# Routing of a grouped top-2 MoE on one core: fewer steps for group scores and counts, lists moved, router weights loaded a stage earlier

## The chip, the core and the metric

The kernel runs on one NeuronCore of a Trainium2 chip. The metric is device time of one execution in microseconds (us). Engines: TensorE (PE), VectorE (DVE), ScalarE (ACT), GpSimd (POOL) and SyncE (SP), each with its own instruction stream; they meet through semaphores.

## The reference

One inference step of a two-layer decoder trunk, all in fp32: a gated linear attention layer, then a differential attention layer, for 512 prompt tokens and 8 sample tokens together. Each layer ends with a mixture of experts of 16 experts in 4 groups, and this is what the change is about:

```python
probs = softmax((xt @ w_router + b_router).astype(float32), axis=-1)
pg = probs.reshape(-1, N_GROUPS, EXPERTS_PER_GROUP)          # 4 groups of 4
gscore = sum(lax.top_k(pg, 2)[0], axis=-1)                   # score of a group: its two best
gidx = argmax(gscore, axis=-1)
in_group = take_along_axis(pg, gidx[:, None, None], axis=1)[:, 0]
vals, idx = lax.top_k(in_group, 2)
wts = vals / sum(vals, axis=-1, keepdims=True)
...
for e in range(16):
    h = silu(xt @ w_gate[e]) * (xt @ w_up[e])
    y = y + comb[:, e:e + 1] * (h @ w_down[e])
```

## The kernel before

The kernel is a row of stages, each a block of one program per engine; a block ends with a barrier of all engines. Tokens lie in tiles of 128 partitions, NTT = 5 of them (four of the prompt, one with the 8 sample tokens). For each layer the stages around the change are the same: the mixer's output projection, `stage_modulate` (L339), `stage_route` (L1121), `stage_experts` (L1367), `stage_combine` (L1572).

`stage_modulate` scales and shifts the rows of each tile on VectorE (L377, L380), turns them on TensorE (L389), copies them on ScalarE (L399) and stores the rows from SP's queue (L359). Two row buffers take turns, so VectorE's tile i waits until the store of tile i - 2 has landed. SP first issues the loads of the gate rows (L335, L336). The argument `ahead` names further loads, which SP issues behind the gate rows and before the first row store; in this stage of before it is empty.

`stage_route` begins on SP with the router's weights (L1160, 64 bytes a piece) and bias (L1161), then the two vectors of the layer norm (L1162, L1163), then 2 MB each of gate, up and down weights of expert 0 and gate and up of expert 1 (L1117). TensorE waits for weights and bias, and for VectorE's memset of the weights' padding (L1235). It multiplies them with the tokens (L1195, four shares in parallel), ScalarE and VectorE take the shares out of PSUM, TensorE adds them (L1200). From there VectorE works through a chain of small instructions, nearly each followed by a drain (`tt`, L1229, is a TENSOR_TENSOR and a drain): softmax, group scores as the maximum over six pairs of experts (11 instructions), the mask of the best group (the last of its steps at L1279), first and second choice (O1, O2). Then choices are masked with `valid` (rows past the 8 sample tokens), summed to T, and added up tile by tile in `before`. TensorE turns the counts into each choice's rank within its expert (L1206 to L1209). VectorE works out how many tiles of 128 slots each expert needs (`nt`, L1298 to L1303) and where they start (a scan, L1306), and the slot of each choice (RK). Next come the lists for the expert stage, on one partition: which expert a late tile belongs to (`m.texp`), which tiles are more than half full (`m.full`), and how many pairs of tiles run; they are read by `stage_experts` only. Then the slots (`m.dest`), ten one-hot matrices (L1361), of which TensorE makes the token list as each comes (L1213), and the copy of that list, `m.idx` (L1364), which ends the stage.

`stage_experts` runs over slot tiles: GpSimd gathers the rows named in `m.idx` (L1420, L1423), TensorE turns them (L1436), multiplies with gate and up weights (L1488) and down weights (L1470). SP loads the weights for tile n once the gate and up product of tile n - 2 is done (L1117).

Of the kernel before, what the change touches and what calls it, by code (L numbers as in the profile page):

```python
# [1120 lines left out]
def stage_route(nc, ctx, m, l, a, weights):  # L1121
# [3 lines left out]
    w_in, ln_in, tab, mm, ev, sel_ok, rk_mm, hot_ok, idx_mm, tri_ok = (sem(n) for n in  # L1125
        ("w_in", "ln_in", "tab", "mm", "ev", "sel_ok", "rk_mm", "hot_ok", "idx_mm", "tri_ok"))
    ex_ok, wz_ok, sh_mm, sh_cp = (sem(n) for n in ("ex_ok", "wz_ok", "sh_mm", "sh_cp"))
    off = [2 * D]
# [5 lines left out]
    wr, br = take(KT, 32), take(1, NE)[:, 0, :]  # L1134
    shares = take(1, SEQ + 32)[:, 0, :]
    before = take(NTT + 1, NE)
    L, E, O1, O2, T, RK = (take(NTT, NE) for _ in range(6))
    GS, GM = take(NTT, NG), take(NTT, NG)
    A1, A2, A3 = (take(NTT, 1)[:, :, 0] for _ in range(3))
# [17 lines left out]
    with nc.Block() as block:  # L1157
        @block.sync
        def _(sp):
            sp.dma_start(wr[:, :, 0:NE], a["w_router"].rearrange("(p k) n -> p k n", k=KT)).then_inc(w_in, 16)  # L1160
            sp.dma_start(br, a["b_router"].partition_broadcast(P)).then_inc(w_in, 16)  # L1161
            sp.dma_start(m.lnr[:, 0, :], a["ln_ffn_g"][l].partition_broadcast(P)).then_inc(ln_in, 16)  # L1162
            sp.dma_start(m.lnr[:, 1, :], a["ln_ffn_b"][l].partition_broadcast(P)).then_inc(ln_in, 16)  # L1163
            load_expert(sp, m, weights, 0, 0)
            load_expert(sp, m, weights[0:2], 1, 1)
            sp.wait_ge(ln_in, 32)

        @block.gpsimd
        def _(g):
# [16 lines left out]
            nc.gpsimd.iota(row0, pattern=[[1, P]], base=-P, channel_multiplier=0, allow_small_or_imprecise_dtypes=True).then_inc(tab, 1)  # L1186

        @block.tensor
        def _(pe):
            pe.wait_ge(w_in, 32)  # L1190
            pe.wait_ge(wz_ok, 1)
            for k in range(KT):
                g = k % 4
                for bank, t0, n in ((m.ps[0], 0, SEQ), (m.ps[1], SEQ, 32)):
                    last = nc.tensor.matmul(bank[32 * g:32 * g + 32, 0:n], wr[:, k, :], m.xt[:, k, t0:t0 + n],  # L1195
                                            start=(k < 4), stop=(k >= 4), tile_position=(0, 32 * g))
            last.then_inc(sh_mm, 1)
            pe.wait_ge(sh_cp, 2)
            for i, r in TILES:
                last = nc.tensor.matmul(m.ps[2][0:r, i * NE:(i + 1) * NE], shares[:, i * P:i * P + r], m.fold[:, 0:NE],  # L1200
                                        start=True, stop=True)
            last.then_inc(mm, 1)
            pe.wait_ge(sel_ok, 1)
            pe.wait_ge(tab, 10)

            nc.tensor.matmul(m.ps[3][:, 0:NTT * NE], m.ones[:, :], before[:, 0:NTT, :].rearrange("p i e -> p (i e)"),  # L1206
                             start=True, stop=False)
            nc.tensor.matmul(m.ps[3][:, 0:NTT * NE], tri, T.rearrange("p i e -> p (i e)"), start=False, stop=True)
            last = nc.tensor.matmul(m.ps[5][:, 0:NE], m.ones[:, :], before[:, NTT, :], start=True, stop=True)  # L1209
# [15 lines left out]
        def _(v):  # L1225
# [11 lines left out]
            V.memset(before[:, 0, :], 0.0)  # L1237
# [21 lines left out]
            pairs = [(x, y) for x in range(EPG) for y in range(x + 1, EPG)]  # L1259
# [4 lines left out]
            v.wait_ge(tab, 10)  # L1264
# [12 lines left out]
            tt(E.rearrange("p i (g e) -> p i g e", e=EPG), e4, GM.unsqueeze(3).to_broadcast([P, NTT, NG, EPG]), ALU.mult)  # L1277
            tt(E.rearrange("p i (g e) -> p i g e", e=EPG), e4, GM.unsqueeze(3).to_broadcast([P, NTT, NG, EPG]), ALU.add)
            V.tensor_scalar(E, E, -1.0, None, ALU.add)  # L1279
# [10 lines left out]
            tt(O1, O1, bc(valid), ALU.mult)  # L1290
            tt(O2, O2, bc(valid), ALU.mult)
            tt(T, O1, O2, ALU.add)
            for i in range(NTT):
                tt(before[:, i + 1, :], before[:, i, :], T[:, i, :], ALU.add)
            v.nop().then_inc(sel_ok, 1)
            v.wait_ge(rk_mm, 1)

            V.tensor_scalar(nt, m.ps[5][:, 0:NE], float(P), None, ALU.is_gt)  # L1298
            v.drain()
            for c in range(2, NTT):  # L1300
                V.tensor_scalar(tmp16, m.ps[5][:, 0:NE], float(c * P), None, ALU.is_gt)
                v.drain()
                tt(nt, nt, tmp16, ALU.add)  # L1303
            V.memset(zero16, 1.0)
# [13 lines left out]
            tt(RK, RK, far, ALU.add)  # L1318

# [25 lines left out]
            for c, O in enumerate((O1, O2)):  # L1345
                tt(O, O, RK, ALU.mult)
                V.tensor_reduce(out=slot[:, c, :], in_=O, axis=AX.X, op=ALU.add)
                v.drain()
                V.tensor_copy(m.dest[:, c, :], slot[:, c, :])
            slot1 = slot.rearrange("p c i -> p (c i)")  # L1350
            tt(reached, slot1.unsqueeze(2).to_broadcast([P, NJ, SLOT_TILES + 1]),
               tile0.unsqueeze(1).to_broadcast([P, NJ, SLOT_TILES + 1]), ALU.is_ge)
            V.tensor_reduce(out=row, in_=reached, axis=AX.X, op=ALU.add)
            V.tensor_tensor(token_at, reached[:, :, 0:SLOT_TILES], reached[:, :, 1:SLOT_TILES + 1], ALU.subtract)

            tt(tok, tok, valid, ALU.mult)
            V.scalar_tensor_tensor(out=row, in0=row, scalar=float(-P), in1=slot1, op0=ALU.mult, op1=ALU.add)
            by_choice = token_at.rearrange("p (c i) t -> p c i t", i=NTT)
            tt(by_choice, by_choice, tok.unsqueeze(1).unsqueeze(3).to_broadcast([P, 2, NTT, SLOT_TILES]), ALU.mult)
            for j in range(NJ):  # L1360
                V.tensor_scalar(row_hot[:, j, :], row0, row[:, j:j + 1], None, ALU.is_equal).then_inc(hot_ok, 1)  # L1361

# [1048 lines left out]
def build(nc, a):  # L2411
    held.clear()
    with ExitStack() as ctx:
# [46 lines left out]
```

## Time and profile before

| | us |
|---|---|
| median of three runs | 2049.24 |
| lowest and highest of them | 2048.81 and 2052.35 |
| the profiled execution | 2054.24 |
| its span in the trace | 2052.4 |

| engine | busy us | share of the span |
|---|---|---|
| PE | 1583.4 | 77% |
| PEld (weight load, beside PE) | 729.2 | 36% |
| DVE | 753.0 | 37% |
| ACT | 390.5 | 19% |
| POOL | 364.8 | 18% |

HBM traffic is 274 GB/s over the span. Times of the trace are microseconds from the start of the span. Layer 0's modulation begins at about 500 us and its routing at 516, layer 1's routing at 1583. A row of the timeline gives the start, the duration, the engine, the line, the operation with its tiles and shapes, and how many instructions it merges; in brackets stands the engine's idle time before it and what ended it. A drain isn't counted as busy, so the time from one start to the next is more than the duration where a drain lies between, and can be less where none does. PEclk is TensorE's granted clock as a share of 2.4 GHz, so 0.50 is 1.2 GHz. The DMA share is the mean busy share of the core's 16 DMA engines.

### The profile page before, as it was taken

To read this page: it belongs to the slowest core of one execution; us is meant where nothing else is said; L and a number is where in the kernel's file an instruction comes from. 1 tells how busy PE (TensorE), PEld (TensorE's weight loads), DVE (VectorE), ACT (ScalarE), POOL (GpSimd) and SP (SyncE) were. 2 spreads that over 40 slices of the span, in tenths; PEclk is the share of its full clock that TensorE was granted. 3 is DMA by queue.
4 is the path that set the end of the run, shared out by engine and by line. 5 is a ranking of instruction groups with operands and counts; after the bars stand their busy time and mean duration, and the time that the engine had idled before them with its cause. 6 is when DMAs were issued, how large, how long until landed. Compare 5 with 4: busy or idle time off the path is not lost. (4 is left out here: it accounts for less than half of the span.)

```text
span 2052.4 us, 22129 instructions
## 1 busy us (share of the span) xinstructions
PE 1583.4 (77%) x7466; PEld 729.2 (36%) x7467; DVE 753.0 (37%) x1314; ACT 390.5 (19%) x755; POOL 364.8 (18%) x274
## 2 busy tenths in 40 slices
PE   6999976786288998946889887777495399989950
PEld 2333335233133333312346563344342233333320
DVE  1010134575400000036755568995455400000008
ACT  1010022011022122222120002333211011222212
POOL 0000000001010000023735566650001000000004
PEclk8989987588589999977999998889796599999985
DMA  8652620611589989969969999884402579999972
GB/s 330 256 198 84 245 84 12 229 71 52 238 329 428 376 352 425 427 275 328 362 225 378 405 389 411 336 319 139 185 21 82 224 291 386 409 428 428 428 296 92
DMA packets 122909, 563.03 MB, mean 274 GB/s; under 512 B 13621, under 2 KB 43126, under 8 KB 101307
## 3 DMA queue, kind: packets, MB, share of 16 engines
q1 hardware_dynamic: 98450, 496.63, 61.0%
q10 hardware_dynamic: 15424, 33.08, 4.2%
q0 software_dynamic: 8944, 32.15, 4.2%
q8 instruction: 51, 0.84, 0.2%
q14 instruction: 40, 0.33, 0.0%
HBM read 521.80 MB, written 40.03 MB: 274 GB/s over the span
## 5 line engine op out<-in xcount | busy, mean ns | idle before, releaser
L1488 PE MATMUL ps<-arena_w,arena_r 128*64 128x512 f32 x1664 | 378.6, 612 | 33.5 <-issue 28.5
L1488 PEld LDWEIGHTS ps<-arena_w,arena_r 128*64 128x64 f32 x1664 | 126.4, 141 | 279.4 <-issue 273.3
L1470 PE MATMUL ps<-arena_w,arena_r 128*64 128x512 f32 x832 | 186.9, 597 | 19.2 <-ACT arena_r L1518 19.2
L1565 DVE TENSOR_TENSOR arena_r<-arena_r,ps 128x512 f32<-128x512 f32 x38 | 26.2, 688 | 441.9 <-ACT arena_r L1535 441.9
L1868 POOL TENSOR_TENSOR arena_w<-arena_w,arena_r 128x1024 f32<-128x1024 f32 x48 | 116.4, 2430 | 112.5 <-DMA arena_w<-in_cache_k_dram 111.9
L1921 PE MATMUL ps<-arena_w,xt 128*128 128x256 f32 x512 | 124.3, 405 | 1.4 <-ACT xt L2086 1.4
L1868 POOL TENSOR_TENSOR arena_r<-arena_r 128x1024 f32<-128x1024 f32 x48 | 115.0, 2400 | 48.9 <-DMA arena_r<-in_cache_k_dram 48.8
L512 PE MATMUL ps<-arena_w,xt 128*128 128x512 f32 x256 | 113.6, 601 | 0.4 <-PE ps L206 0.4
L1091 POOL TENSOR_TENSOR x_res<-x_res,arena_m 128x1024 f32<-128x1024 f32 (+1 forms) x20 | 52.6, 2631 | 341.6 <-DVE x_res L1085 341.6
L1022 PE MATMUL ps<-arena_w,xt 128*128 128x512 f32 x256 | 111.1, 593 | 0.0
L1921 PEld LDWEIGHTS ps<-arena_w,xt 128*128 128x128 f32 x512 | 103.0, 204 | 18.2 <-ACT xt L2086 1.5
L1420 POOL COPY small<-idx 128x1 int32 (+1 forms) x38 | 6.9, 183 | 567.2 <-PE ps L1436 485.5
L1470 PEld LDWEIGHTS ps<-arena_w,arena_r 128*64 128x64 f32 x832 | 56.8, 137 | 123.1 <-issue 101.4
L1558 DVE COPY arena_r<-ps 128x512 f32<-128x512 f32 x38 | 26.3, 692 | 192.1 <-PE ps L1470 192.1
L1534 ACT ACTIVATE arena_r<-ps 64x512 f32<-64x512 f32 x38 | 22.4, 588 | 360.3 <-PE ps L1488 360.3
L2237 DVE TENSOR_REDUCE arena_r<-arena_w 128x16 f32<-128x1024 f32 x64 | 76.8, 1213 | 25.9 <-POOL arena_w L1868 25.8
L2237 DVE TENSOR_REDUCE arena_r<-arena_r 128x16 f32<-128x1024 f32 x64 | 76.6, 1210 | 16.5 <-POOL arena_r L1868 16.5
L1933 PE MATMUL ps<-arena_m,arena_r 128*16 128x512 f32 x512 | 68.8, 661 | 6.1 <-DMA arena_m<-in_cache_v_dram 6.1
L512 PEld LDWEIGHTS ps<-arena_w,xt 128*128 128x128 f32 x256 | 48.3, 192 | 66.7 <-issue 66.7
L1022 PEld LDWEIGHTS ps<-arena_w,xt 128*128 128x128 f32 x256 | 48.2, 190 | 60.0 <-issue 58.4
L471 PE MATMUL ps<-xt,arena_w 128*128 128x512 f32 x128 | 58.7, 612 | 4.0 <-PEq L248 3.7
L1913 PE MATMUL ps<-xt,arena_w 128*128 128x512 f32 x128 | 60.3, 630 | 0.0
(355 smaller groups left out, 1959.1 us busy)
## 6 DMA issues: line engine op xcount, KB each, us to landing
arena_w<-in_w_exp_gate_dram SPq DMA_DIRECT2D x38, 2048.0 KB, 13.4
arena_w<-in_w_exp_up_dram SPq DMA_DIRECT2D x38, 2048.0 KB, 17.2
arena_w<-in_w_exp_down_dram SPq DMA_DIRECT2D x38, 2048.0 KB, 18.9
arena_m<-in_cache_v_dram SPq DMA_DIRECT2D x128, 512.0 KB, 8.3
arena_w<-in_cache_k_dram SPq DMA_DIRECT2D x64, 512.0 KB, 8.3
arena_r<-in_cache_k_dram SPq DMA_DIRECT2D x64, 512.0 KB, 9.8
arena_w<-in_w_ada_dram SPq DMA_DIRECT2D x12, 2048.0 KB, 16.8
arena_m<-in_w_ada_dram SPq DMA_DIRECT2D x12, 2048.0 KB, 8.5
```

The source lines that it names most:

```text
L471: last = nc.tensor.matmul(m.ps[n % 2][:, :], w, m.xt[:, k, 0:SEQ], start=(k == 0), stop=(k == KT - 1))
L512: last = nc.tensor.matmul(m.ps[4 + n % 4][:, :], m.xt[:, k, i * P:(i + 1) * P], m.wr[c % 2][:, k, :], start=(k == 0), stop=(k == KT - 1))
L1022: last = nc.tensor.matmul(m.ps[(4 if n % 2 else 6) + c][0:r, :], m.xt[:, k, i * P:i * P + r], w[:, k, c * 512:(c + 1) * 512], start=(k == ...
L1091: nc.gpsimd.tensor_tensor(m.x[0:r, i, :], m.x[0:r, i, :], m.lnr[0:r, 1, :], ALU.add).then_inc(self.done, 1)
L1470: last = nc.tensor.matmul(psy[c][at:at + 64, :], ht[u][:, k, 64 * (1 - a):64 * (2 - a)], wd[u][:, k, c * 512:(c + 1) * 512], start=(k == 0 ...
L1488: last = nc.tensor.matmul(ps[at:at + 64, :], xgt[u][:, k, 64 * a:64 * (a + 1)], w[u][:, k, :], start=(k == 0), stop=(k == KT - 1), tile_po ...
L1558: V.tensor_copy(ys[u][:, 0:512], psy[0][:, :]).then_inc(y_v, 1)
L1868: G.tensor_tensor(kp[n % RING], kp[n % RING], qb[b % 2], ALU.mult).then_inc(pp_ok, 1)
L1913: last = nc.tensor.matmul(bank[:, :], w[:, k, part * P:(part + 1) * P], m.xt[:, k, 0:SEQ], start=(k == 0), stop=(k == KT - 1))
L1921: last = nc.tensor.matmul(bank[:, i * CW:(i + 1) * CW], m.xt[:, k, t], w[:, k, :], start=(k == 0), stop=(k == KT - 1))
L1933: last = nc.tensor.matmul(PSO[n][32 * g:32 * g + C, :], PR[b % 2][:, GRP * q + g, :], vp[GRP * (v % 2) + g][:, n * 512:(n + 1) * 512], sta ...
L2237: V.tensor_reduce(out=S[b % 2][:, j, :], in_=kp[n % RING].rearrange("p (c d) -> p c d", d=DHB), axis=AX.X, op=ALU.add).then_inc(ks_ok, 1)
```

## The change

Six edits, all for both layers.

- A class `Router` holds the router's weights, bias and their semaphore. Their two loads move from the head of `stage_route` into `stage_modulate`'s `ahead`.
- Group scores: within each group, two couples of experts; the larger of each couple, added, against the larger of the two couples' sums. Five instructions, two of them not followed by a drain, take the place of eleven.
- The mask's last step is folded into the one before it.
- T is masked once in place of O1 and O2. `before` is now laid out with tiles innermost, and one TENSOR_TENSOR_SCAN over 16 x 6 elements fills it; a table `fresh` restarts it for each expert. TensorE reads `before` and the masked T with a stride.
- `nt` comes from one comparison with a table `steps` and one reduction. The table is one more iota on POOL; three more memsets stand at the head of VectorE's part, and one there moves from the chain.
- The block of the lists for the expert stage stands behind the one-hot matrices and before the wait for the token list.

```diff
+class Router:
+    def __init__(self, nc, ctx, m, l, a):
+        self.w_in = ctx.enter_context(m_semaphore(nc, f"route{l}_w_in"))
+        self.wr, self.br = view(m.R, 2 * D, KT, 32), m.R[:, 2 * D + KT * 32:2 * D + KT * 32 + NE]
+        self.ahead = [(self.wr[:, :, 0:NE], a["w_router"].rearrange("(p k) n -> p k n", k=KT), self.w_in),
+                      (self.br, a["b_router"].partition_broadcast(P), self.w_in)]
...
         @block.sync
         def _(sp):
-            sp.dma_start(wr[:, :, 0:NE], a["w_router"].rearrange("(p k) n -> p k n", k=KT)).then_inc(w_in, 16)
-            sp.dma_start(br, a["b_router"].partition_broadcast(P)).then_inc(w_in, 16)
...
-            nc.tensor.matmul(m.ps[3][:, 0:NTT * NE], m.ones[:, :], before[:, 0:NTT, :].rearrange("p i e -> p (i e)"),
+            nc.tensor.matmul(m.ps[3][:, 0:NTT * NE], m.ones[:, :], before[:, :, 0:NTT].rearrange("p e i -> p i e"),
                              start=True, stop=False)
...
-            V.memset(before[:, 0, :], 0.0)
+            V.memset(chosen, 0.0)
+            V.memset(fresh, 1.0)
+            v.drain()
+            V.memset(fresh[:, :, 0:1], 0.0)
+            V.memset(zero16, 1.0)
...
-            for n, (x, y) in enumerate(pairs):
-                tt(G3 if n else GS, e4[:, :, :, x], e4[:, :, :, y], ALU.add)
-                if n:
-                    tt(GS, GS, G3, ALU.max)
+            V.tensor_tensor(hi, two[:, :, :, 0], two[:, :, :, 1], ALU.max)
+            tt(both, two[:, :, :, 0], two[:, :, :, 1], ALU.add)
+            V.tensor_tensor(gs, hi[:, :, 0], hi[:, :, 1], ALU.add)
+            tt(g3, both[:, :, 0], both[:, :, 1], ALU.max)
+            tt(gs, gs, g3, ALU.max)
...
-            V.tensor_scalar(E, E, -1.0, None, ALU.add)
+            V.scalar_tensor_tensor(out=e4, in0=GM.unsqueeze(3).to_broadcast([P, NTT, NG, EPG]), scalar=-1.0, in1=e4,
+                                   op0=ALU.add, op1=ALU.add)
...
-            tt(O1, O1, bc(valid), ALU.mult)
-            tt(O2, O2, bc(valid), ALU.mult)
             tt(T, O1, O2, ALU.add)
-            for i in range(NTT):
-                tt(before[:, i + 1, :], before[:, i, :], T[:, i, :], ALU.add)
-            v.nop().then_inc(sel_ok, 1)
+            tt(taken, T, bc(valid), ALU.mult)
+            V.tensor_tensor_scan(before.rearrange("p e i -> p (e i)"), fresh.rearrange("p e i -> p (e i)"),
+                                 chosen.rearrange("p e i -> p (e i)"), 0.0, ALU.mult, ALU.add).then_inc(sel_ok, 1)
+            v.drain()
             v.wait_ge(rk_mm, 1)
 
-            V.tensor_scalar(nt, m.ps[5][:, 0:NE], float(P), None, ALU.is_gt)
-            v.drain()
-            for c in range(2, NTT):
-                V.tensor_scalar(tmp16, m.ps[5][:, 0:NE], float(c * P), None, ALU.is_gt)
-                v.drain()
-                tt(nt, nt, tmp16, ALU.add)
-            V.memset(zero16, 1.0)
+            tt(over, m.ps[5][:, 0:NE].unsqueeze(2).to_broadcast([P, NE, NTT - 1]), steps.unsqueeze(1).to_broadcast([P, NE, NTT - 1]),
+               ALU.is_gt)
+            V.tensor_reduce(out=nt, in_=over, axis=AX.X, op=ALU.add)
             v.drain()
...
-            one = cmp_[0:1, 0:MORE, :]
-            tt(one, end[0:1].unsqueeze(1).to_broadcast([1, MORE, NE]), tix[0:1, 0:MORE].unsqueeze(2).to_broadcast([1, MORE, NE]), ALU.is_le)
...
-            V.tensor_copy(m.texp[0:1, SLOT_TILES:SLOT_TILES + 1], tmp16[0:1, 0:1])
             for c, O in enumerate((O1, O2)):
                 tt(O, O, RK, ALU.mult)
...
             for j in range(NJ):
                 V.tensor_scalar(row_hot[:, j, :], row0, row[:, j:j + 1], None, ALU.is_equal).then_inc(hot_ok, 1)
 
+            one = cmp_[0:1, 0:MORE, :]
+            tt(one, end[0:1].unsqueeze(1).to_broadcast([1, MORE, NE]), tix[0:1, 0:MORE].unsqueeze(2).to_broadcast([1, MORE, NE]), ALU.is_le)
...
+            V.tensor_copy(m.texp[0:1, SLOT_TILES:SLOT_TILES + 1], tmp16[0:1, 0:1])
             v.wait_ge(idx_mm, 1)
             V.tensor_copy(m.idx[:, :], m.ps[4][:, 0:SLOT_TILES])
...
-        stage_modulate(nc, ctx, m, "ffn0", 3, 3, have=2, keep_rows=True)
+        router = Router(nc, ctx, m, 0, a)
+        stage_modulate(nc, ctx, m, "ffn0", 3, 3, have=2, keep_rows=True, ahead=router.ahead)
         weights = expert_weights(nc, ctx, m, 0, a)
-        stage_route(nc, ctx, m, 0, a, weights)
+        stage_route(nc, ctx, m, 0, a, weights, router)
```

## Rows read from the trace of the kernel before

**Rows 1.** Windows of layer 0: us of each engine, clock, DMA share, GB/s
```profile
515.90:557.00 41.10, 11.02 (x68) 8.03 (x68) 21.01 (x107) 2.14 (x3) 1.39 (x12) 0.54 0.70 283
...
547.00:548.00 1.00, 0.00 (x0) 0.00 (x0) 0.78 (x6) 0.00 (x0) 0.00 (x0) 0.50 0.08 33
...
576.30:620.00 43.70, 36.24 (x174) 15.29 (x174) 4.13 (x6) 12.09 (x23) 3.60 (x7) 0.96 0.99 404
```

**Rows 2.** Timeline, routing of layer 0: start, duration, engine, operation [idle before]
```profile
515.92 0.56 SPq L1160 DMA_DIRECT2D arena_r<-in_w_router_dram  x1
...
516.01 0.17 DVE L1235 MEMSET arena_r<- 128x128 f32 x1 [2.31 <-PEq L347]
...
517.23 0.59 SPq L1162 DMA_DIRECT2D arena_m<-in_ln_ffn_g_dram  x1
...
519.38 3.89 PE L1195 MATMUL ps<-xt,arena_r 128*32 128x512 f32 x32 [4.59 <-DMA arena_r<-in_b_router_dram]
...
523.99 1.20 PE L1200 MATMUL ps<-fold,arena_r 128*128 128x16 f32 x10 [0.71 <-ACT arena_r L1220]
```

**Rows 3.** Timeline, routing of layer 1
```profile
1586.70 3.89 PE L1195 MATMUL ps<-xt,arena_r 128*32 128x512 f32 x32 [4.66 <-DMA arena_r<-in_b_router_dram]
...
1591.31 2.04 PE L1200 MATMUL ps<-fold,arena_r 128*128 128x16 f32 x10 [0.72 <-ACT arena_r L1220]
```

**Rows 4.** Timeline, modulation of layer 0
```profile
502.97 11.04 SPq L359 DMA_DIRECT2D xm_rows<-arena_r  x5
...
505.92 1.23 DVE L377 SCALAR_TENSOR_TENSOR arena_r<-arena_m,x_res 128x1024 f32<-128x1024 f32 x1 [0.53 <-DMA xm_rows<-arena_r]
```

**Rows 5.** Windows: the queue before the row store; router weights alone
```profile
503.30:503.70 0.40, 0.40 (x3) 0.40 (x2) 0.40 (x1) 0.00 (x0) 0.00 (x0) 0.50 0.28 113
...
517.00:518.30 1.30, 0.00 (x0) 0.00 (x0) 0.00 (x0) 0.00 (x0) 0.37 (x3) 0.50 0.59 60
```

**Rows 6.** Timeline, selection and counts, layer 0
```profile
527.13 3.13 DVE L1229 TENSOR_TENSOR arena_r<-arena_r 128x80 f32<-128x80 f32 x12
...
532.22 0.20 DVE L1279 TENSOR_SCALAR arena_r<-arena_r 128x80 f32<-128x80 f32 x1
...
537.20 2.12 DVE L1229 TENSOR_TENSOR arena_r<-arena_r 128x80 f32<-128x80 f32 x8
...
539.40 0.71 PE L1206 MATMUL ps<-arena_r,ones 128*128 128x80 f32 x2 [14.21 <-DVEq L1230]
```

**Rows 7.** Timeline, VectorE behind the counts' products, layer 0
```profile
540.90 0.17 DVE L1298 TENSOR_SCALAR arena_r<-ps 128x16 f32<-128x16 f32 x1 [1.58 <-PE ps L1209]
...
542.84 0.19 DVE L1306 TENSOR_TENSOR_SCAN arena_r<-arena_r 128x16 f32<-128x16 f32 x1
...
543.36 0.24 DVE L1310 TENSOR_SCALAR arena_r<-ps 128x80 f32<-128x80 f32 x1
...
543.51 0.17 DVE L1311 SCALAR_TENSOR_TENSOR arena_r<-arena_r 128x16 f32<-128x16 f32 x1
```

**Rows 8.** Timeline, lists, one-hot rows and token list, layer 0
```profile
544.15 0.91 DVE L1229 TENSOR_TENSOR arena_r<-arena_r 128x80 f32<-128x80 f32 x3
...
548.24 0.22 DVE L1229 TENSOR_TENSOR arena_r<-arena_r 128x80 f32<-128x80 f32 x1
...
551.55 2.05 DVE L1361 TENSOR_SCALAR arena_r<-arena_r 128x128 f32<-128x128 f32 x10
...
556.39 0.18 DVE L1364 CAST idx<-ps 128x24 int32<-128x24 f32 x1 [2.79 <-PE ps L1213]
```

**Rows 9.** Timeline, first products of layer 0's expert stage
```profile
566.55 8.65 PE L1488 MATMUL ps<-arena_w,arena_r 128*64 128x512 f32 x28 [1.16 <-ACT arena_r L1512]
...
576.27 0.36 SPq L1117 DMA_DIRECT2D arena_w<-in_w_exp_gate_dram  x1
...
578.45 7.09 PE L1488 MATMUL ps<-arena_w,arena_r 128*64 128x512 f32 x32 [1.31 <-ACT arena_r L1512]
```

**Rows 10.** Groups by line: the other scan, busy us, mean ns
```profile
L650 DVE TENSOR_TENSOR_SCAN arena_r<-arena_r 128x512 f32<-128x512 f32 x4 | 4.9, 1214 | 0.0
```

More of the change, by code:

```diff
@@ L1118, in load_expert, with stage_route @@
                      source[bass.ds(e, 1)].rearrange("a (p k) n -> p (a k n)", k=k)).then_inc(loaded[u], 16)
-def stage_route(nc, ctx, m, l, a, weights):
+class Router:
[4 more added lines that the diff above has]
+                      (self.br, a["b_router"].partition_broadcast(P), self.w_in)]
+def stage_route(nc, ctx, m, l, a, weights, router):
     sem = lambda n: ctx.enter_context(m_semaphore(nc, f"route{l}_{n}"))
-    w_in, ln_in, tab, mm, ev, sel_ok, rk_mm, hot_ok, idx_mm, tri_ok = (sem(n) for n in
-        ("w_in", "ln_in", "tab", "mm", "ev", "sel_ok", "rk_mm", "hot_ok", "idx_mm", "tri_ok"))
+    ln_in, tab, mm, ev, sel_ok, rk_mm, hot_ok, idx_mm, tri_ok = (sem(n) for n in
+        ("ln_in", "tab", "mm", "ev", "sel_ok", "rk_mm", "hot_ok", "idx_mm", "tri_ok"))
+    w_in, wr, br = router.w_in, router.wr, router.br
     ex_ok, wz_ok, sh_mm, sh_cp = (sem(n) for n in ("ex_ok", "wz_ok", "sh_mm", "sh_cp"))
-    off = [2 * D]
+    off = [2 * D + KT * 32 + NE]
     def take(*shape):
@@ L1133, in take @@
         return v
-    wr, br = take(KT, 32), take(1, NE)[:, 0, :]
     shares = take(1, SEQ + 32)[:, 0, :]
-    before = take(NTT + 1, NE)
     L, E, O1, O2, T, RK = (take(NTT, NE) for _ in range(6))
+    before, fresh, chosen = (take(NE, NTT + 1) for _ in range(3))
+    taken = chosen[:, :, 1:].rearrange("p e i -> p i e")
     GS, GM = take(NTT, NG), take(NTT, NG)
+    HI, PS = take(2 * NTT, NG), take(2 * NTT, NG)
+    over, steps = take(NE, NTT - 1), take(1, NTT - 1)[:, 0, :]
     A1, A2, A3 = (take(NTT, 1)[:, :, 0] for _ in range(3))
@@ L1186, in _ @@
             nc.gpsimd.iota(row0, pattern=[[1, P]], base=-P, channel_multiplier=0, allow_small_or_imprecise_dtypes=True).then_inc(tab, 1)
+            nc.gpsimd.iota(steps, pattern=[[P, NTT - 1]], base=P, channel_multiplier=0, allow_small_or_imprecise_dtypes=True).then_inc(tab, 1)
         @block.tensor
@@ L1203, in _ @@
             pe.wait_ge(sel_ok, 1)
-            pe.wait_ge(tab, 10)
-            nc.tensor.matmul(m.ps[3][:, 0:NTT * NE], m.ones[:, :], before[:, 0:NTT, :].rearrange("p i e -> p (i e)"),
+            pe.wait_ge(tab, 11)
+            nc.tensor.matmul(m.ps[3][:, 0:NTT * NE], m.ones[:, :], before[:, :, 0:NTT].rearrange("p e i -> p i e"),
                              start=True, stop=False)
-            nc.tensor.matmul(m.ps[3][:, 0:NTT * NE], tri, T.rearrange("p i e -> p (i e)"), start=False, stop=True)
-            last = nc.tensor.matmul(m.ps[5][:, 0:NE], m.ones[:, :], before[:, NTT, :], start=True, stop=True)
+            nc.tensor.matmul(m.ps[3][:, 0:NTT * NE], tri, taken, start=False, stop=True)
+            last = nc.tensor.matmul(m.ps[5][:, 0:NE], m.ones[:, :], before[:, :, NTT], start=True, stop=True)
             last.then_inc(rk_mm, 1)
@@ L1258, in _ @@
             e4 = E.rearrange("p i (g e) -> p i g e", e=EPG)
-            pairs = [(x, y) for x in range(EPG) for y in range(x + 1, EPG)]
-            for n, (x, y) in enumerate(pairs):
-                tt(G3 if n else GS, e4[:, :, :, x], e4[:, :, :, y], ALU.add)
-                if n:
-                    tt(GS, GS, G3, ALU.max)
-            v.wait_ge(tab, 10)
+            two = E.rearrange("p i (g q e) -> p (i g) q e", q=2, e=2)
+            hi, both = (x.rearrange("p i g -> p (i g)").rearrange("p (n q) -> p n q", q=2) for x in (HI, PS))
+            gs, g3 = (x.rearrange("p i g -> p (i g)") for x in (GS, G3))
+            V.tensor_tensor(hi, two[:, :, :, 0], two[:, :, :, 1], ALU.max)
[3 more added lines that the diff above has]
+            tt(gs, gs, g3, ALU.max)
+            v.wait_ge(tab, 11)
             def first_of(onehot, score, best, weights, n):
@@ L1275, in _ @@
             first_of(GM, GS, A1, w4, NG)
[L1277 to L1279 removed]
+            tt(e4, e4, GM.unsqueeze(3).to_broadcast([P, NTT, NG, EPG]), ALU.mult)
+            V.scalar_tensor_tensor(out=e4, in0=GM.unsqueeze(3).to_broadcast([P, NTT, NG, EPG]), scalar=-1.0, in1=e4,
+                                   op0=ALU.add, op1=ALU.add)
             v.drain()
@@ L1318, in _ @@
             tt(RK, RK, far, ALU.add)
+            for c, O in enumerate((O1, O2)):
+                tt(O, O, RK, ALU.mult)
+                V.tensor_reduce(out=slot[:, c, :], in_=O, axis=AX.X, op=ALU.add)
+                v.drain()
+                V.tensor_copy(m.dest[:, c, :], slot[:, c, :])
+            slot1 = slot.rearrange("p c i -> p (c i)")
+            tt(reached, slot1.unsqueeze(2).to_broadcast([P, NJ, SLOT_TILES + 1]),
+               tile0.unsqueeze(1).to_broadcast([P, NJ, SLOT_TILES + 1]), ALU.is_ge)
+            V.tensor_reduce(out=row, in_=reached, axis=AX.X, op=ALU.add)
+            V.tensor_tensor(token_at, reached[:, :, 0:SLOT_TILES], reached[:, :, 1:SLOT_TILES + 1], ALU.subtract)
+            tt(tok, tok, valid, ALU.mult)
+            V.scalar_tensor_tensor(out=row, in0=row, scalar=float(-P), in1=slot1, op0=ALU.mult, op1=ALU.add)
+            by_choice = token_at.rearrange("p (c i) t -> p c i t", i=NTT)
+            tt(by_choice, by_choice, tok.unsqueeze(1).unsqueeze(3).to_broadcast([P, 2, NTT, SLOT_TILES]), ALU.mult)
+            for j in range(NJ):
+                V.tensor_scalar(row_hot[:, j, :], row0, row[:, j:j + 1], None, ALU.is_equal).then_inc(hot_ok, 1)
             one = cmp_[0:1, 0:MORE, :]
@@ L1344, in _ @@
             V.tensor_copy(m.texp[0:1, SLOT_TILES:SLOT_TILES + 1], tmp16[0:1, 0:1])
[L1345 to L1361, printed above, removed]
             v.wait_ge(idx_mm, 1)
@@ L2434, in build @@
                          (a["ln_mix_g"][1], a["ln_mix_b"][1]), 8, 9, w_at=8192)
-        stage_modulate(nc, ctx, m, "ffn1", 9, 3, have=2, keep_rows=True)
+        router = Router(nc, ctx, m, 1, a)
+        stage_modulate(nc, ctx, m, "ffn1", 9, 3, have=2, keep_rows=True, ahead=router.ahead)
         weights = expert_weights(nc, ctx, m, 1, a)
-        stage_route(nc, ctx, m, 1, a, weights)
+        stage_route(nc, ctx, m, 1, a, weights, router)
         stage_experts(nc, ctx, m, 1, weights)
```

## The prediction

> **What bounds the kernel now.** I read three views in this order. First the stages. The kernel is a row of stages with barriers between them. Layer 0's routing stage is a stretch of 41 us with TensorE at 11 us of work and VectorE at 21 us [rows 1]. Nothing is large there: it is a chain of small dependent instructions, and its length goes into the span in full if the stage behind it waits for its end. Second, the timeline of that stretch: what starts it, what each link costs from start to start, and where VectorE stands idle [rows 2, 3, 6 to 8]. Third, whether the expert stage behind would absorb a shorter routing. Expert weights preloaded by routing have landed by 547 us (DMA share 0.08 from there) [rows 1], but the first product needs the token list, which is ready at 556.4 [rows 8], and runs from 566.55; SP asks for the next weights only when that product is done, at 576.27 [rows 9]. From there DMA is 0.99 busy [rows 1]. So the DMA-bound part begins when routing lets it, and every microsecond taken out ahead of the token list moves it. Both layers have the same chain; I cost layer 0 and double it.
>
> **Part A, router weights loaded by the modulation stage.** Before, TensorE's first routing product starts at 519.38 behind the bias load, and VectorE's memset, its other condition, is done at 516.18 [rows 2]; in layer 1, where it starts at 1586.70, TensorE idles 4.66 us for the same load, against 4.59 [rows 2, 3]. Without the loads the product follows the memset by some 0.05 us: 519.38 - 516.23 = 3.15 us. VectorE now does two more memsets and a drain behind the first one; they lie beside the 3.89 us of products [rows 2], as does the added iota on POOL, which has 20 us until its tables are used.
>
> What the moved step costs in its new place: two issues on SP, 0.61 + 0.70 us from start to start [rows 2], ahead of the first row store at 502.97, which waits for VectorE anyway [rows 4]. In the code SP has only two gate-row loads ahead of it, so I let the issues fit. Their packets then lie on SP's queue ahead of that store. The router weights are 1024 pieces of 64 bytes; where they are alone, the engines are 0.59 busy for 1.3 us, so 0.77 us of work [rows 5], and the bias (an eighth of the pieces) some 0.2. The queue has a gap of 0.4 us at share 0.28 before the store, worth 0.29 us [rows 5]. VectorE waits 0.53 us for this store's landing before its third tile [rows 4], so a late store delays the stage one for one. Delay: 0.97 - 0.29 = 0.7; in layer 1 the gap is thinner, so I take 0.8. Ends: 0 (the pieces go into other unused slots) and 1.4 (the 1.3 us of wall time plus a bit of bias, no overlap). In return SP reaches the gain vectors and expert weights 1.3 us sooner (517.23 against 515.92) [rows 2], of no value with the slack of 9 us found above. **A = 3.15 - 0.8 = 2.35.**
>
> The Trainium skill ("DMA: Bandwidth & Descriptors", section "Queues, rings and completion order") says that each DMA engine takes its descriptors in ring order. By that rule the store can't pass the router pieces, and the delay is nearer 1.0 than 0; if it were fully serial, the total below would be 0.4 us smaller in all.
>
> **Part B, couples in place of pairs.** Twelve drained TENSOR_TENSORs take 3.13 us, 0.26 each [rows 6]; eleven are the six pairs: 2.87. In their place stand five, of which two are followed with no drain. A drained 40- or 20-element one costs 0.28 and 0.26 twice; an undrained one starts its follower after 0.15 us at 80 elements (543.36 to 543.51) [rows 7], so about 0.10 and 0.08 here. 2.87 - 0.98 = **1.89**. Ends: 2.0, and 1.53 if the undrained ones cost full price.
>
> [...]
>
> **Part C**, one TENSOR_SCALAR folded into a neighbour: 0.20 us, and a gap of 0.08 as between the last drained one (537.20 + 2.12) and what follows it at 539.40 [rows 6]: **0.28**.
>
> **Part D, one scan for the counts.** From 537.20 eight drained operations run until TensorE starts at 539.40: 2.20 us [rows 6]. After: two 80-element ones (three of about that size take 0.91, so 0.31 each [rows 8]), one now with a strided output, and one scan over 96 elements. A scan over 16 takes 0.19 and starts at 542.84 [rows 7], one over 512 takes 1.21 [rows 10]: 2.06 ns an element, so 0.36. With 0.08 to TensorE: 1.06. **D = 1.14**, between 0.95 and 1.3. TensorE's operands are now strided; I take nothing for it (up to 0.15).
>
> **Part E, tiles of an expert.** From 540.90 to the scan at 542.84: 1.94 us for seven small operations and a memset [rows 7]. After: one 64-element comparison and one reduction, both drained: 0.29 each. **E = 1.36** (1.3 to 1.45).
>
> **Part F, late tiles' lists moved.** They begin with the third operation of the group at 544.15, so at 544.77, and end at 548.24 [rows 8]: 3.47 us on the chain. Behind the ten one-hot rows VectorE stands idle 2.79 us until TensorE's twenty products are done at 556.39 [rows 8]. The lists start at about 553.55 and end at 553.55 + 3.47 = 557.02, so the copy of the token list, queued behind them, comes 0.63 us later than TensorE would let it. What is late next is therefore VectorE, not TensorE. The stage's barrier and then the gathers wait for it; the cover is worth 2.8 us, and were it gone the move would bring nothing. **F = 3.47 - 0.63 = 2.84** (2.6 to 3.0).
>
> **Sum.** 2.35 + 1.89 + 0.28 + 1.14 + 1.36 + 2.84 = 9.86 a layer, 19.7 for two. The profiled execution took 2054.24 us (span 2052.4), 5 us above the median of three, 2049.24. It would come to 2034.5, the median to 2049.24 - 19.7 = **2029.5**. By the lower ends (A 1.75, B 1.53, C 0.2, D 0.95, E 1.3, F 2.6) the gain is 8.3 a layer, 16.7 in all; by the upper ones (3.15, 2.0, 0.3, 1.3, 1.45, 3.0) it is 11.2, 22.4 in all.
>
> **Rivals.**
> 1. *TensorE's clock rises sooner.* Routing runs mostly at 1.2 GHz, half clock: 0.54 granted over the stretch [rows 1]. The ten fold products take 2.04 us in layer 1 and 1.20 in layer 0 [rows 3, 2], where the clock came up to 2.4 GHz while they ran. With the 3 us wait gone the first products follow the transposes of modulation more closely. At most 3.89 / 2 = 1.95 a layer and 0.84 for layer 1: 4.7 more, 2024.8. The opposite, layer 0 losing its 0.84, gives 2030.3. In layer 0 the clock came up only when the 32 products that started at 519.38 were through, and in layer 1 not even in the fold products [rows 2, 3], so the early rise is unlikely.
> 2. *The expert stage absorbs it.* If the stream of weights set its pace from the preload on, only SP's earlier start would count, 1.3 - 0.8 = 0.5 a layer, or 1.3 at most: 2046.6 to 2048.2, no change. Against it stand the quiet queue after 547 and the load that waits for the first product [rows 1, 9].
> 3. *The lists are not hidden.* If VectorE's lists delayed the row products too, or ran much slower next to TensorE, F is 0: 2029.5 + 5.7 = 2035.2. Their order in the code speaks against it. The whole change doing nothing would need this and 2.
> 4. *Slower: the clock in the expert stage.* That stage starts at half clock and comes to 0.96 within two tiles [rows 1, 9]. A gate-and-up product of 32 matmuls takes 7.09 us at full clock [rows 9], 14.2 at half. If the changed phase and shorter activity ahead held the clock down, each tile would lose 7.1 us where TensorE is the bound. The gain is eaten from three such tiles (21.3), and it is slower by over 0.2% from four: 2029.5 + 28.4 = 2057.9. Against it stands the 0.96 granted over the 43.7 us from 576.3, after a routing stage that was mostly idle too [rows 1].
>
> **Numbers.** Forecast with its bounds 0.80; rival 1 0.09; rival 2 0.03; rival 3 0.05; rival 4 0.03. The median of three also moves by a microsecond or two (2048.81 to 2052.35 before). Ends: 2049.24 - 22.4 - 2 = 2024.8, which takes in rival 1, rounded to 2024; and 2049.24 - 16.7 + 2 to 3, which takes in rival 3: 2036. About 0.2%, 4.1 us, is what a measurement tells from no change. Faster 0.94 (forecast, rivals 1 and 3), same 0.03, slower 0.03.
>
> **What would show it.** A: the first product some 0.2 us behind the stage's start, and VectorE's wait for the first row store up from 0.53 to about 1.3 us. If it stays at 0.5, A is 3.15. B to E: 0.98 us from the normalised probabilities to the reduction; one scan of 0.36; two operations of 0.58 ahead of the second scan. F: the last list operation, not TensorE, releases the token list, and idle time there is gone. From the token list to the first product and the end of the expert stage all times are as before, less the shift; an expert stage that is longer by what routing lost would prove rival 2, and a longer stretch at 0.5 in it rival 4. I am wrong above all if routing is shorter by 10 us a layer and the span isn't by 20.

## The result and the profile after

| | before | after |
|---|---|---|
| median of four runs, us | 2050.8 | 2033.49 |
| lowest to highest | 2048.81 to 2053.67 | 2031.04 to 2035.83 |
| ratio of runs, 95% interval | | 0.9908 (0.9887 to 0.9929) |
| a second series of the same kernel, five rounds: median | 2057.19 | 2032.99 |
| its ratio, 95% interval | | 0.9881 (0.9855 to 0.9907) |
| profiled execution (its span) | 2054.24 (2052.4) | 2031.04 (2029.2) |

Forecast were 2029.5 us and 19.7 us of gain. Measured are 17.3 us between the medians of the first series and 24.2 between those of the second. The interval of the first series is 14.6 to 23.2 us. The totals of one kernel scatter by several microseconds, so they can't tell 17 from 22. The traces can: VectorE's links of the routing chain repeat to a few hundredths, apart from short idle gaps of some 0.3 to 0.4 us. Four other links move from one execution to the next, and are named where they matter: modulation (by up to 0.8 us in layer 1), the first routing products (by 0.2 in layer 0), the fold products of layer 1 (1.20 or 2.04), and the last stretch to the first expert product (by 0.3).

The head of layer 0's routing stage after the change, in the timeline of all engines (start, duration, engine, line, operation, idle before). It answers [rows 2].

```profile
513.83 0.34 SPq L1172 DMA_DIRECT2D arena_m<-in_ln_ffn_g_dram  x1
513.92 0.17 DVE L1246 MEMSET arena_r<- 128x128 f32 x1 [2.32 <-PEq L347]
...
514.23 3.76 PE L1206 MATMUL ps<-xt,arena_r 128*32 128x512 f32 x32 [1.54 <-DVE arena_r L1246]
...
518.73 1.20 PE L1211 MATMUL ps<-fold,arena_r 128*128 128x16 f32 x10 [0.73 <-ACT arena_r L1231]
```

The first product now waits for VectorE's memset and starts 0.31 us behind the memset's start, where it was 3.37 behind in [rows 2]. The same view further on, for parts B to E; it answers [rows 6] and [rows 7].

```profile
521.87 0.24 DVE L1240 TENSOR_TENSOR arena_r<-arena_r 128x80 f32<-128x80 f32 x1
522.18 0.20 DVE L1277 TENSOR_TENSOR arena_r<-arena_r 128x40 f32<-128x40 f32 x1
522.30 0.19 DVE L1240 TENSOR_TENSOR arena_r<-arena_r 128x40 f32<-128x40 f32 x1
...
523.16 0.18 DVE L1286 TENSOR_REDUCE arena_r<-arena_r 128x5 f32<-128x20 f32 x1
...
529.83 0.62 DVE L1240 TENSOR_TENSOR arena_r<-arena_r 128x80 f32<-128x80 f32 x2
530.52 0.36 DVE L1310 TENSOR_TENSOR_SCAN arena_r<-arena_r 128x96 f32<-128x96 f32 x1
...
530.93 0.72 PE L1217 MATMUL ps<-arena_r,ones 128*128 128x80 f32 x2 [11.01 <-DVE arena_r L1310]
...
532.44 0.22 DVE L1240 TENSOR_TENSOR arena_r<-ps,arena_r 128x64 f32<-128x64 f32 x1 [1.56 <-PE ps L1220]
532.73 0.22 DVE L1317 TENSOR_REDUCE arena_r<-arena_r 128x16 f32<-128x64 f32 x1
533.03 0.19 DVE L1319 TENSOR_TENSOR_SCAN arena_r<-arena_r 128x16 f32<-128x16 f32 x1
```

The couples run from 522.18 to 523.16, 0.98 us for five. The scan over 96 elements takes the 0.36 us that the two others gave by a straight line. From the counts' products to VectorE's next step are 1.51 us, against 1.50 before (539.40 to 540.90): the strided operands of TensorE cost nothing that shows.

The end of the stage, VectorE alone but for two rows of other engines. It answers [rows 8] and the first row of [rows 9].

```profile
538.30 2.05 DVE L1349 TENSOR_SCALAR arena_r<-arena_r 128x128 f32<-128x128 f32 x10
538.64 4.46 PE L1224 MATMUL ps<-arena_r 128*128 128x24 f32 x20 [6.25 <-DVE arena_r L1349]
540.27 0.27 DVE L1240 TENSOR_TENSOR arena_r<-arena_r 1x128 f32<-1x128 f32 x1
...
543.66 0.14 DVE L1375 CAST texp<-arena_r 1x1 int32<-1x1 f32 x1
543.73 0.16 DVE L1377 CAST idx<-ps 128x24 int32<-128x24 f32 x1
...
553.84 9.47 PE L1501 MATMUL ps<-arena_w,arena_r 128*64 128x512 f32 x32 [1.16 <-ACT arena_r L1525]
```

The copy of the token list has no idle time before it any more. TensorE's products were through at 543.10; the lists, 3.46 us long, hold the copy until 543.73.

The chain cut at the same points in both kernels, start to start, from the timelines:

| stretch | layer 0 before | after | layer 1 before | after |
|---|---|---|---|---|
| modulation to the head of routing | 15.59 | 16.09 | 16.08 | 16.90 |
| to the first routing product | 3.37 | 0.31 | 3.46 | 0.31 |
| to the shares' copy | 3.97 | 3.86 | 3.97 | 3.95 |
| to the reciprocal (fold products, softmax) | 3.51 | 3.51 | 4.35 | 3.51 |
| to the first selection (part B) | 3.47 | 1.56 | 3.81 | 1.56 |
| to the counts' products (C, D) | 9.07 | 7.77 | 8.80 | 7.79 |
| to the scan for starts (E) | 3.44 | 2.10 | 3.44 | 2.09 |
| to the one-hot rows (F, the part saved) | 8.71 | 5.27 | 9.02 | 5.27 |
| to the copy of the token list (F, given back) | 4.84 | 5.43 | 4.84 | 5.43 |
| to the first expert product | 10.16 | 10.11 | 9.80 | 9.78 |
| **sum** | 66.13 | 56.01 | 67.57 | 56.59 |

The chains are shorter by 10.12 and 10.98 us, 21.1 in all. The spans of these two executions differ by 23.2: the part before layer 0's modulation is 2.6 us shorter in the one after, with nothing changed there, and the two other stretches (first expert product to layer 1's modulation, and from layer 1's first expert product to the end) are 0.4 and 0.1 longer.

### The profile page after: what moved, and what is told of

It reads as the page before. It is cut to its first block and busy times, and to the rows that moved or that the text cites. A ratio compares the mean times of both kernels' runs of the same rounds, so it can differ in the third digit from the quotient of the medians.

```text
span 2029.2 us, 22063 instructions
## 1 busy us (share of the span) xinstructions
PE 1577.2 (78%) x7466; PEld 725.8 (36%) x7467; DVE 748.1 (37%) x1284; ACT 390.9 (19%) x755; POOL 365.0 (18%) x276
## 5 line engine op out<-in xcount | busy, mean ns | idle before, releaser
L2250 DVE TENSOR_REDUCE arena_r<-arena_w 128x16 f32<-128x1024 f32 x64 | 76.8, 1212 | 23.2 <-POOL arena_w L1881 23.1
L2250 DVE TENSOR_REDUCE arena_r<-arena_r 128x16 f32<-128x1024 f32 x64 | 76.7, 1210 | 17.0 <-POOL arena_r L1881 16.9
## 6 DMA issues: line engine op xcount, KB each, us to landing
arena_w<-in_w_exp_gate_dram SPq DMA_DIRECT2D x38, 2048.0 KB, 14.6
```

Source lines behind the costliest of these rows:

```text
L2250: V.tensor_reduce(out=S[b % 2][:, j, :], in_=kp[n % RING].rearrange("p (c d) -> p c d", d=DHB), axis=AX.X, op=ALU.add).then_inc(ks_ok, 1)
```

## The experiments

The theory was that the routing chain goes into the span one for one, part by part as in the sum. The rival was that the expert stage gives some of it back. Each run was compared in its total and by the same stretches, with "chain" for the sum of both layers' chains. The 95% interval of a kernel's ratio reaches some 0.0026 to either side, which makes some 7.6 us for the difference of two kernels: the medians below agree or disagree with a theory only loosely, and the stretches decide. The same kernel run again has a chain of 55.94 + 56.07 = 112.0 us, and the one of the table above 112.6.

**again.** The changed kernel, unedited.

> The changed kernel as it is, for a closer ratio. Theory 1 (what leaves the routing chain leaves the span one for one): the two profiled executions differ by 10.1 us in layer 0 and 11.0 us in layer 1 between the start of modulation and the first expert product, so 21.1 us or a ratio of 0.9897. Theory 2 (the expert stage or a later one gives some of it back, since the medians of four runs differ by 17.3 us only): 0.9915 or closer to 1, and in the new profile a longer time from the first expert product to the end of the stage. In the trace: 56.0 and 56.6 us from the start of modulation to the first product.

Its ratio is 0.9881 (0.9855 to 0.9907), nearer to the first theory; 0.9897 lies within both series' intervals, 0.9915 only in the first one's. From the first expert product of layer 0 to the next modulation it takes 1000.7 us, before 1000.6: nothing is given back there.

**no_a.** Part A undone.

```diff
+            for buf, src, loaded in router.ahead:
+                sp.dma_start(buf, src).then_inc(loaded, 16)
             sp.dma_start(m.lnr[:, 0, :], a["ln_ffn_g"][l].partition_broadcast(P)).then_inc(ln_in, 16)
...
-        stage_modulate(nc, ctx, m, "ffn0", 3, 3, have=2, keep_rows=True, ahead=router.ahead)
+        stage_modulate(nc, ctx, m, "ffn0", 3, 3, have=2, keep_rows=True)
```

> The changed kernel with the router's loads back at the head of the routing stage, all else kept. Theory 1: the first routing product starts 3.4 us behind the stage's start again and modulation is shorter by 0.5 us in layer 0 and 0.8 us in layer 1, so 2.7 and 2.3 us more: 5.0 us above the changed kernel. If layer 1's fold products go back to 2.0 us from 1.2 as TensorE starts later behind the transposes (the clock), 5.9 us. Theory 2: about 2 us, the earlier issue of the expert weights alone.

Median 2037.79, 4.8 us above the changed kernel. Its chain is 118.3 us, 6.3 above the second execution of the changed kernel. 3.17 a layer came back at the products, 0.3 and 0.8 left modulation, 0.2 is the first products of layer 0 (3.97 from start to the copy, against 3.73), and 0.84 the fold products of layer 1. Expected were 5.0, or 5.9 with slow fold products. The timeline of TensorE in layer 1's routing, of this kernel:

```profile
1584.56 3.89 PE L1208 MATMUL ps<-xt,arena_r 128*32 128x512 f32 x32 [4.67 <-DMA arena_r<-in_b_router_dram]
...
1589.17 2.04 PE L1213 MATMUL ps<-fold,arena_r 128*128 128x16 f32 x10 [0.72 <-ACT arena_r L1233]
```

and of "again":

```profile
1572.34 3.89 PE L1206 MATMUL ps<-xt,arena_r 128*32 128x512 f32 x32 [1.50 <-DVE arena_r L1246]
...
1576.93 1.20 PE L1211 MATMUL ps<-fold,arena_r 128*128 128x16 f32 x10 [0.70 <-ACT arena_r L1231]
```

**no_f.** Part F undone: the block of lists stands ahead of the slots again.

> The changed kernel with the lists back ahead of the slots, all else kept. Theory 1: 3.45 us more ahead of the one-hot rows and 0.6 us less behind them, 2.85 a layer, 5.7 us in all; TensorE releases the token list again after 2.8 us of idle time. Theory 2: less than 3 us in all.

Median 2040.18, 7.2 above. The chain is 118.4, 6.4 above: 3.45 us more ahead of the one-hot rows and 0.59 less behind them in each layer, and again 0.84 of layer 1's fold products, which ran slow in this execution though the loads were early. The timeline of VectorE, layer 0:

```profile
544.35 2.05 DVE L1374 TENSOR_SCALAR arena_r<-arena_r 128x128 f32<-128x128 f32 x10
549.19 0.18 DVE L1377 CAST idx<-ps 128x24 int32<-128x24 f32 x1 [2.79 <-PE ps L1224]
```

The wait of 2.79 us for TensorE is back as in [rows 8]. 5.7 of 6.4 are what was expected of the part itself.

**no_bcde.** Parts B to E undone, with the five additions on the new layout. Of the edit, part D:

```diff
-            tt(T, O1, O2, ALU.add)
-            tt(taken, T, bc(valid), ALU.mult)
-            V.tensor_tensor_scan(before.rearrange("p e i -> p (e i)"), fresh.rearrange("p e i -> p (e i)"),
-                                 chosen.rearrange("p e i -> p (e i)"), 0.0, ALU.mult, ALU.add).then_inc(sel_ok, 1)
-            v.drain()
+            tt(O1, O1, bc(valid), ALU.mult)
+            tt(O2, O2, bc(valid), ALU.mult)
+            tt(taken, O1, O2, ALU.add)
+            for i in range(NTT):
+                tt(before[:, :, i + 1], before[:, :, i], chosen[:, :, i + 1], ALU.add)
+            v.nop().then_inc(sel_ok, 1)
```

> The changed kernel with the six pairs, the mask's third step, the five additions (on the new layout) and the seven small operations for tiles back, all else kept. Theory 1: 1.91 + 0.28 + 1.10 + 1.35 = 4.64 a layer, 9.3 us in all. Theory 2: less than 5 us in all. The additions read and write with a stride now; if a stride costs VectorE anything they take more than 0.26 us each from start to start.

Median 2037.04, only 4.1 above. That is the rival's side, but the theory's 9.3 is only 5.2 away and so within the 7.6 us too. The trace decides against the rival: the chain is 122.2, 10.2 above. B is 1.91 and 2.26 us, E 1.35 and 1.35, as expected, and C and D together 1.53 and 1.15; with 0.84 for the slow fold products. The execution profiled hides 5.5 of these 10.2 us in stretches that the edit doesn't touch: outside the chains it took 1912.2 us, and "again" 1917.7. Whether the other five runs did the same isn't known, as they have no trace. A stride costs VectorE little here: the eight operations with strided ones among them take 2.25 us, before 2.12 [rows 6].

**longer.** Time added to the chain.

```diff
             tt(taken, T, bc(valid), ALU.mult)
+            for _ in range(20):
+                tt(far, O1, O2, ALU.add)
```

> The changed kernel with twenty more drained operations of 128x80 on VectorE's chain, ahead of the counts (results overwritten later). Theory 1 (what the chain takes goes into the span one for one): 20 x 0.31 = 6.2 us a layer between the first selection and the counts' products, 12.4 us in all, and from the first expert product to the next stage no change beyond the scatter. Theory 2 (the expert stage absorbs a part, as its weights stream is the bound): less than 8 us in all, and a shorter stretch from the first expert product to the next layer's modulation.

Median 2047.22, 14.2 above the 2032.99 of "again", which was of another series; by the ratios (0.9967 against 0.9881 and 0.9908) it is 17.7 and 12.1 us. The group of operations in the timeline of VectorE, layer 0:

```profile
531.16 6.95 DVE L1240 TENSOR_TENSOR arena_r<-arena_r 128x80 f32<-128x80 f32 x22
```

Twenty more take 6.33 us (6.95 against 0.62), 12.7 in both layers, and the chain grew by 13.2: the fold products of layer 1 ran slow (0.84), and modulation took 0.2 less. From layer 0's first expert product to the next modulation it took 1001.2 us, against 1000.7: the expert stage absorbs nothing of a longer chain. With the 1000.7 of "again" against 1000.6 before, for a shorter one, this settles rival 2 of the prediction in both directions.

**behind.** The router's loads behind the first row store.

```diff
-            for buf, src, loaded in ahead:
-                sp.dma_start(buf, src).then_inc(loaded, 16)
             if keep_rows:
                 for i, r in TILES:
                     sp.wait_ge(xm_ok, i + 1)
                     sp.dma_start(m.xmD[i * P:i * P + r, :], xm[i % 2][0:r, :]).then_inc(rows_out[i % 2], 16)
+                    if i == 0:
+                        for buf, src, loaded in ahead:
+                            sp.dma_start(buf, src).then_inc(loaded, 16)
```

> The changed kernel with the router's two loads issued behind the first row store of modulation in place of ahead of it. Theory 1 (the store of tile 0 lies behind the router's pieces on SP's queue, and VectorE's third tile waits for it): VectorE's wait goes back from 1.0 and 1.9 us to 0.5 and 1.1, and modulation from 16.1 and 16.4 to 16.9 us back to 15.6 and 16.1, with the first routing product still 0.3 us behind the stage's start; 1.1 us less in all. Rival (the pieces cost engine time wherever they stand): the wait for the second row store, zero so far, grows to 0.5 us or more, and modulation stays at 16.1 us or above.

Modulation took 15.78 and 16.02 us. The starts of VectorE's first, third and fourth tile in layer 1, in the timeline of "behind":

```profile
1555.34 1.22 DVE L378 SCALAR_TENSOR_TENSOR arena_r<-arena_m,x_res 128x1024 f32<-128x1024 f32 x1
...
1558.85 1.23 DVE L378 SCALAR_TENSOR_TENSOR arena_r<-arena_m,x_res 128x1024 f32<-128x1024 f32 x1 [1.00 <-DMA xm_rows<-arena_r]
...
1561.69 1.23 DVE L378 SCALAR_TENSOR_TENSOR arena_r<-arena_m,x_res 128x1024 f32<-128x1024 f32 x1 [0.32 <-DMA xm_rows<-arena_r]
```

Both theories were half right. The wait for the first store is shorter (0.71 and 1.00), but the second store, free of any wait before, now makes VectorE wait 0.14 in layer 0 and 0.32 in layer 1; the wait for the last tile, 0.3 before, is 0.07 and 0. Median 2033.77, ratio 0.9904 (0.9872 to 0.9937): not to be told from the changed kernel by its total.

**actq.** The same loads from ScalarE's own queue; one execution.

```diff
-            for buf, src, loaded in ahead:
-                sp.dma_start(buf, src).then_inc(loaded, 16)
...
         @block.scalar
         def _(s):
+            for buf, src, loaded in ahead:
+                s.dma_start(buf, src).then_inc(loaded, 16)
```

> The changed kernel with the router's two loads issued by ScalarE, idle then, at the start of modulation, on its own DMA queue. Theory 1 (order on one queue makes the delay): modulation takes 15.6 and 16.1 us as before, or less than a quarter of a microsecond more. Rival (it is the engines' work that delays the store, whichever queue the pieces are on): 16.1 us and more, with VectorE's wait for the first row store at 1.0 us or above. What the late issue on SP costs in layer 1 (the bias load took SP 1.76 us, and the first store went out 0.5 us late) is gone under both.

Modulation took 15.98 and 17.00 us, with waits for the first row store of 0.93 and 1.98. In layer 1, timeline of VectorE:

```profile
1558.73 1.23 DVE L375 SCALAR_TENSOR_TENSOR arena_r<-arena_m,x_res 128x1024 f32<-128x1024 f32 x1 [1.98 <-DMA xm_rows<-arena_r]
```

The pieces stood on another queue, no store was behind them, and SP issued the first store on time. The store still landed late. So the order on one queue isn't needed for a delay; the rival, the work of the shared engines, fits. It is one execution, so the size stays rough, and the cause is argued by what is left over and not shown directly. Its total of 2027.77 us, the lowest of all here, tells nothing of the edit: its chain is 112.7 us, and outside the chains it took 1913.2.

**best.** The loads as in "behind", and the lists with independent steps side by side: five drains in place of ten (the expectation miscounts them as six and twelve).

```diff
+            V.tensor_tensor(one, wide(end), tall, ALU.is_le)
+            V.scalar_tensor_tensor(out=lim[0:1], in0=m.ps[5][0:1, 0:NE], scalar=1.0 / P, in1=start[0:1], ...)
+            V.tensor_scalar(tef[0:1, MORE:MORE + half], tix[0:1, 0:MORE:2], end[0:1, NE - 1:NE], None, ALU.is_lt)
+            v.drain()
+            V.tensor_reduce(out=tef[0:1, 0:MORE], in_=one, axis=AX.X, op=ALU.add)
...
```

> The changed kernel with the loads behind the first row store and the lists written so that independent steps stand side by side: six drains in place of twelve, with undrained neighbours. Theory 1: 0.5 and 0.6 us less in modulation; the lists take 2.4 us in place of 3.47 and so fit into the 2.8 us in which TensorE makes the token list, which TensorE then releases again: 4.84 us from the first one-hot row to the copy in place of 5.43. 1.1 us a layer, 2.2 in all, near the limit of what the totals can tell. Rival: undrained neighbours cost what drained ones do, the lists still take 3 us or more, and the 5.4 us stay.

VectorE's timeline, layer 0:

```profile
538.92 0.27 DVE L1356 TENSOR_TENSOR arena_r<-arena_r 1x128 f32<-1x128 f32 x1
539.12 0.15 DVE L1357 SCALAR_TENSOR_TENSOR arena_r<-ps,arena_r 1x16 f32<-1x16 f32 x1
539.21 0.21 DVE L1358 TENSOR_SCALAR arena_r<-arena_r 1x4 f32<-1x4 f32 x1
...
541.52 0.16 DVE L1375 CAST full<-arena_r 1x8 int32<-1x8 f32 x1
541.80 0.18 DVE L1377 CAST idx<-ps 128x24 int32<-128x24 f32 x1
```

The lists take 2.8 us, not 2.4, and just fit: 4.84 us from the first one-hot row to the copy in both layers, the 0.59 back. Modulation took 15.98 and 15.79 us, 0.1 and 0.6 less than in "again", where 0.5 and 0.6 were expected: with the same place of the loads as in "behind", layer 0 gained little. The chain is 110.9 us, 1.1 below "again" though the fold products of layer 1 ran slow (0.84), and 22.8 below before. In the total that can't be seen: median 2032.96, ratio 0.9899 (0.9873 to 0.9925), level with the changed kernel.

## Why the prediction was right, point by point

**What bounds it** was read rightly: a chain whose length goes into the span in full. "longer" shows the slope: 13.2 us more in the chain, 12 to 18 in the total by either series, and the stretch from the first expert product on unchanged.

**A**, 2.35 a layer. The first product came 3.06 and 3.15 us closer to the stage's start, as the 3.15 of the sum. The price in modulation was taken as 0.8. The two profiles give 0.50 and 0.82, but over all executions modulation took 15.6 to 15.8 us in layer 0 with the loads elsewhere (before, "no_a") and 16.1 to 16.3 with them ahead; in layer 1 15.6 to 16.1 against 16.1 to 16.9. That is 0.5 in the mean, so this term was mis-sized by 0.3 a layer. The place was right: the wait of VectorE's third tile for the first row store grew from 0.53 to 1.01 in layer 0 and from 1.07 to 1.89 in layer 1. The reason given was queue order, and "actq" speaks against it as the only cause: a queue of its own didn't take the delay away. In layer 1 most of it was another thing, SP itself: the bias load held SP 1.76 us, and the store went out 3.10 us behind modulation's start instead of 2.55.

```profile
1555.53 0.57 SPq L355 DMA_DIRECT2D arena_r<-in_w_router_dram  x1
1556.14 1.76 SPq L355 DMA_DIRECT2D arena_r<-in_b_router_dram  x1
...
1557.95 11.81 SPq L359 DMA_DIRECT2D xm_rows<-arena_r  x5
```

(timeline of the changed kernel). These 0.55 us are two thirds of layer 1's 0.82. From the store's issue to VectorE's third tile layer 1 took 3.46 to 3.54 us in four of the five executions with the loads ahead and 3.75 in this one, against 3.48 and 3.05 in the two with the loads elsewhere; in layer 0 it took 3.43 to 3.61 against 2.95 and 3.11. So the delay that the prediction describes is plain in layer 0, and in layer 1 it is at most half a microsecond and hard to tell from the scatter. "The issues fit" was true in layer 0 only.

**B**, 1.89: measured 1.91, and 2.25 in layer 1, where an idle gap of 0.43 us inside the pairs, in which VectorE waited for nothing that the profile shows, went with them. The couples took the 0.98 of the sum. The undrained one of 0.20 us was followed after 0.12 us (522.18 to 522.30), so it started before the one ahead of it was done. The Trainium skill ("VectorE: DVE Perf Modes", section "The DRAIN you can't avoid") says that the next operation waits for the pipe to be empty, but that "a next op that is not held starts earlier"; the trace shows the second here.

**C and D**, 0.28 + 1.14 = 1.42: measured 1.30 and 1.01 for the stretch. D alone is 2.20 - 1.10 = 1.10, and C alone 0.29 (from 531.33 to 532.50 before, four operations with the mask's last one [rows 6], and 0.88 us for three after). What is missing to 1.39 is idle gaps of the kind just named: one of 0.34 us stood in this stretch in layer 0 before and none in layer 1, and after the change one of about 0.42 stands in each layer ahead of a RECIPROCAL:

```profile
529.09 0.19 DVE L1304 RECIPROCAL arena_r<-arena_r 128x5 f32<-128x5 f32 x1 [0.41 <-issue]
```

**E**, 1.36: measured 1.34 and 1.35. **F**, 2.84: measured 3.44 - 0.59 = 2.85 in layer 0, and 3.16 in layer 1, which had such a gap (0.21) before as well. The prediction's "what is late next is VectorE" is what the trace shows, and "no_f" gives the part back.

**The sum**, 9.86 a layer, stands against 10.12 and 10.98. In layer 0 the 0.26 are mostly the cheaper modulation and first products that took 0.11 less. The excess of 1.12 in layer 1 is mostly the **first rival** in small: its fold products ran in 1.20 us in place of 2.04, worth 0.84; gaps are the rest. The 0.84 was priced rightly. In layer 0 the fold products ran in 1.2 us in all profiles. In layer 1 they did so in three of the eight with the loads ahead of the stage (the profiled one after, "again", "actq") and in neither of the two with the loads in it. So this part of the 21.1 us is luck of the execution profiled: with slow fold products it would be 20.3. The three are among the four of the ten executions in which layer 1's modulation took longest (16.39 to 16.99 us), so a part of what was lost there came back; why wasn't settled. The 32 products ahead of them never took less than 3.69 us in place of 3.97 (start to the shares' copy), so the 1.95 of that rival did not come.

**The second rival** (absorbed) fell with "longer". **The third** (lists not hidden) fell with the trace and "no_f". **The fourth** (clock in the expert stage) did not come: from layer 1's first expert product to the end it took 417.7 us against 417.6, and from layer 0's to the next modulation 1001.0 against 1000.6.

The forecast was 4.0 us below the median of the first series. The chains gained 1.4 us more than the 19.7 forecast. So what the totals lack isn't in the chains: outside them the ten executions profiled took between 1912 and 1926 us, and before's own median was 2049.24 over the three runs of the forecast, 2050.8 over four, 2057.19 in the second series and 2053.42 in a third. That the total fell inside the forecast's range rests on these as much as on the sum; the sum is borne out by the stretches.

## What to carry to other kernels

A chain of small dependent instructions ahead of a stage that can't start without it was worth its full length here, though the stage behind is bound by DMA, because that stage's next weight loads waited for its first product and so for the chain. Look for that wait first; adding time to the chain is a cheap test of it. Work that only a later stage needs goes behind the point where another engine takes over, and then its length against that engine's time decides what is given back. With edits of a few microseconds in a kernel whose total scatters by more, compare stretches between fixed points of the traces, and trust the total only for the sum.

## What was not expected

- The router's small loads, moved beside the row stores, made modulation longer whether they stood ahead of the first store on the same queue (0.5 us in the mean) or on another queue (0.93 and 1.98 us of wait, against 0.53 and 1.07 before and 0.70 and 0.64 in "no_a"). Behind the first store they cost less (15.78 and 16.02, 15.98 and 15.79 us in the two kernels that had them there), with a part of it on the second store (up to 0.35 us).
- The issue of the bias load held SP for 0.65 us at the head of routing before, and in layer 1's modulation for 1.76, 1.49, 1.47, 1.10 and 1.10 us in five executions. Modulation there took 16.90, 16.40, 16.39, 16.07 and 16.05 us in the same order: where SP is held longer, the first row store goes out later, and at 1.10 us modulation is as long as before (16.08).
- VectorE's idle gaps, in which it waits for nothing that the profile shows, stand at other places once instructions are taken out: 0.34 us in layer 0 and 0.43 and 0.21 in layer 1 before, 0.41 and 0.43 after. What makes them wasn't looked into.
- What makes the untouched stretches differ by up to 14 us from one execution to another was not looked into and stays open. In "no_a" 8 of them lie between layer 0's first expert product and layer 1's modulation (1008.5 us against 1000.7).
